# Differential attention in a two-layer trunk: the query split on all 128 partitions into a tile of its own, and eight copies in place of four

## The reference

```python
q, k, v = jnp.split(u @ w_in, 3, axis=-1)
q = apply_rope(q.reshape(bsz, seq, DIFF_HEADS, 2, DIFF_DH), cos, sin)   # 8 heads, 2 components of 64
k = apply_rope(k.reshape(bsz, seq, DIFF_HEADS, 2, DIFF_DH), cos, sin)
...
s = jnp.einsum('bhcqd,bhckd->bhcqk', qb, k).astype(jnp.float32) * scale
p = jax.nn.softmax(jnp.where(mask, s, -jnp.inf), axis=-1)               # causal mask
a = p[:, :, 0] - lam_val * p[:, :, 1]
return jnp.einsum('bhqk,bhkv->bhqv', a.astype(v.dtype), v)
```

## Time and profile before

| what | value |
|---|---|
| runs | 2237.3, 2237.4, 2239.85 us, median 2237.4 |
| profiled execution | 2239.56 us, of which the span of the trace is 2237.8 us |
| mean granted TensorE clock | 0.998 of 2.4 GHz |
| busy of PE, VectorE, ScalarE, GpSimd | 99%, 73%, 43%, 39% of the span |
| chain of waits that ended last | PE 95%, VectorE 3%, ScalarE 1% |
| attention | about 1078 to 1540 us of the span, 56.9 us a head |

### The profile page before, as it was taken

How to read it: one execution, slowest core, us unless ns; L and a number is a source line. 1 busy time by engine, 2 the same in 40 slices (tenths; PEclk the granted TensorE clock), 3 DMA queues, 4 the chain that set the end, 5 groups by cost and what they waited for, 6 DMA issues and landing times.

```text
span 2237.8 us, 28701 instructions
## 1 busy us (share of the span) xinstructions
PE 2208.1 (99%) x10501; PEld 1836.4 (82%) x10501; DVE 1638.5 (73%) x2141; ACT 973.3 (43%) x1613; POOL 874.3 (39%) x805
## 2 busy tenths in 40 slices
PE   8999999999999999999999999999999999999998
PEld 6888888888888888888888888877888888888887
DVE  6877776599669478399577777786599569388397
ACT  6354454354244243345254445564354243343346
POOL 4945546200234233230866666675201234232320
PEclk9999999999999999999999999999999999999999
DMA  8677743463551632701522222222463542633601
GB/s 256 217 269 259 244 155 99 139 246 113 188 188 43 254 128 103 269 13 38 160 67 66 66 66 66 66 76 76 160 230 109 200 176 75 245 113 123 234 0 76
DMA packets 139844, 317.37 MB, mean 142 GB/s; under 512 B 8609, under 2 KB 82514, under 8 KB 126546
## 3 DMA queue, kind: packets, MB, share of 16 engines
q1 hardware_dynamic: 137552, 315.78, 40.9%
q10 hardware_dynamic: 2178, 0.06, 0.1%
HBM read 242.41 MB, written 56.62 MB: 134 GB/s over the span
## 4 chain that ended last, share of the span: by engine, by line
PE 95%; DVE 3%; ACT 1%; issue 1%; DMA 0%; ACTq 0%; DVEq 0%
PE aps L1317 10%; PE aps L1321 10%; PE aps L1319 10%; PE mps L1317 4%; PE dps L1317 4%; PE mps L1321 4%; PE dps L1321 4%; PE mps L1319 4%; PE dps L1319 4%; PE dps L1183 4%; PE dps L1185 4%; PE dps L1184 4%; PE dps L1201 3%; PE dps L1203 3%; PE dps L1202 3%; PE mps L1676 2%
## 5 line engine op out<-in xcount | busy, mean ns | idle before, releaser
L1317 PE MATMUL aps<-b_ring,w_hi 128*128 128x512 f32 x640 | 249.3, 390 | 0.0
L1321 PE MATMUL aps<-b_ring,w_hi 128*128 128x512 f32 x640 | 249.0, 389 | 0.0
L1319 PE MATMUL aps<-b_ring,w_lo 128*128 128x512 f32 x640 | 249.0, 389 | 0.0
L1031 POOL TENSOR_TENSOR s_blk<-s_blk,a 128x1024 f32<-128x1024 f32 x24 | 68.6, 2860 | 380.1 <-DVE w_lo L2520 253.8
L2538 DVE TENSOR_TENSOR b_ring<-h,b_ring 128x1024 fp32r<-128x1024 f32 x120 | 206.5, 1728 | 5.6 <-ACT b_ring L1914 5.6
L909 POOL TENSOR_TENSOR w_hi<-w_raw,ones 128x256 fp32r<-128x256 f32 (+1 forms) x133 | 122.7, 952 | 201.1 <-PE dps L1203 103.9
L1023 POOL TENSOR_TENSOR s_blk<-a,a22u 128x1024 f32<-128x1024 f32 x12 | 35.5, 2960 | 325.6 <-DMA a<-in_w_up 318.6
L1317 PE MATMUL aps<-b_ring,a_hi 128*128 128x512 f32 x384 | 149.8, 390 | 0.0
L1319 PE MATMUL aps<-b_ring,a_lo 128*128 128x512 f32 x384 | 149.4, 389 | 0.0
L1321 PE MATMUL aps<-b_ring,a_hi 128*128 128x512 f32 x384 | 149.4, 389 | 0.0
L1317 PEld LDWEIGHTS aps<-b_ring,w_hi 128*128 128x128 f32 x640 | 120.1, 188 | 25.4 <-issue 0.7
(11 more groups left out here) (514 smaller groups left out, 6362.5 us busy)
## 6 DMA issues: line engine op xcount, KB each, us to landing
b_ring<-xs SPq DMA_DIRECT2D x42, 2048.0 KB, 7.9
xs<-b_ring SPq DMA_DIRECT2D x14, 2048.0 KB, 7.9
one_hi<-xm SPq DMA_DIRECT2D x19, 1024.0 KB, 5.0
one_lo<-xm SPq DMA_DIRECT2D x19, 1024.0 KB, 7.3
a<-in_w_up SPq DMA_DIRECT2D x16, 1024.0 KB, 5.3
a<-in_w_down SPq DMA_DIRECT2D x16, 1024.0 KB, 7.9
w_raw<-in_diff_w_in SPq DMA_DIRECT2D x24, 512.0 KB, 4.0
mix_a<-in_mlstm_w_in SPq DMA_DIRECT2D x36, 256.0 KB, 7.8
```

The lines of the kernel that those rows point to most:

```text
L1317: nc.tensor.matmul(to[:, n], wh, ring[:, 0, k], start=new and k == 0, stop=False, skip_group_check=not new)
L1319: nc.tensor.matmul(to[:, n], wl, ring[:, 0, k], start=False, stop=False, skip_group_check=not new)
L1321: last = nc.tensor.matmul(to[:, n], wh, ring[:, 1, k], start=False, stop=(k == 3), skip_group_check=not new)
```

## The change

A new tile `qn` of 128 partitions by 2 by 1024 holds the high part (`qn[:, 0]`) and the low part (`qn[:, 1]`) of the queries, each component in the half where it lies in `a_next`. ScalarE writes the high part by one instruction on 128 partitions, VectorE the low part by another. SP then copies, for each part and each component c, the half of `qn` that holds it into both halves of `q_hi[:, c]` or `q_lo[:, c]`: eight copies of 256 KB per head in place of four. PE waits for all eight. The semaphore `qk_hi` counts three per head instead of four. The keys are split as before.

```diff
--- before.py
+++ after.py
@@ -321,6 +321,7 @@
             k_st = sb("k_st", [P, 2, S], f32r, stack=s)
             ee = sb("ee", [P, 2, S], stack=s)
             at = sb("at", [P, NB, P], stack=s)
+            qn = sb("qn", [P, 2, S], f32r, stack=s)
         rings = {j: sb(f"b_ring{j}", [P, 2, 4, HALF], f32r) for j in (0, 2, 1)}
         b_ring = [rings[j] for j in range(3)]
 
@@ -580,12 +581,14 @@
 
             def repeat_q(hd):
 
-                sp.wait_ge(qk_hi, 4 * hd + 2)
-                for c in range(2):
-                    sp.dma_start(q_hi[MAP[1 - c], c].bitcast(f32), q_hi[MAP[c], c].bitcast(f32)).then_inc(q_repeated, 16)
-                sp.wait_ge(q_lo_ready, hd + 1)
-                for c in range(2):
-                    sp.dma_start(q_lo[MAP[1 - c], c].bitcast(f32), q_lo[MAP[c], c].bitcast(f32)).then_inc(q_repeated, 16)
+                for part, dst in ((0, q_hi), (1, q_lo)):
+                    if part == 0:
+                        sp.wait_ge(qk_hi, 3 * hd + 1)
+                    else:
+                        sp.wait_ge(q_lo_ready, hd + 1)
+                    for c in range(2):
+                        for half in range(2):
+                            sp.dma_start(dst[MAP[half], c].bitcast(f32), qn[MAP[c], part].bitcast(f32)).then_inc(q_repeated, 16)
 
             def staged(i, p):
 
@@ -1630,7 +1633,7 @@
             def attention_start(hd, feed=lambda n: None, first=False):
 
 
-                pe.wait_ge(q_repeated, 64 * hd + 64)
+                pe.wait_ge(q_repeated, 128 * hd + 128)
                 pe.wait_ge(qk_ready, hd + 1)
                 scores(hd, 0, first)
                 feed(FEED)
@@ -2285,11 +2288,10 @@
             first_high_part(2)
             first_high_part(3)
 
-            def split_q(hd, c):
-
-                if c == 0:
-                    act.wait_ge(rot_ready, 2 * hd + 1)
-                nc.scalar.activation(q_hi[MAP[c], c], a_next[MAP[c], 0], ACT.Copy).then_inc(qk_hi, 1)
+            def split_q(hd):
+
+                act.wait_ge(rot_ready, 2 * hd + 1)
+                nc.scalar.activation(qn[:, 0], a_next[:, 0], ACT.Copy).then_inc(qk_hi, 1)
 
             def split_k(hd):
                 act.wait_ge(rot_ready, 2 * hd + 2)
@@ -2332,7 +2334,7 @@
                 elif more:
                     split_k(hd + 1)
                 if s == NB - 1 and more:
-                    split_q(hd + 1, 0)
+                    split_q(hd + 1)
                 act.wait_ge(pv_done, n + 1)
                 if m == 0 and follows:
                     act.wait_ge(oy_done, hd)
@@ -2341,9 +2343,6 @@
                 nc.scalar.activation(acc[:, m % 2, 0:P], mps[:, 0, 3 * P:4 * P], ACT.Square,
                                      scale=small[:, 11, m:m + 1],
                                      accum_out=small[:, 3, m:m + 1]).then_inc(o_out, 1)
-                if s == NB - 1 and more:
-                    split_q(hd + 1, 1)
-
             def early_highs(t):
 
                 act.wait_ge(oy_out, 2 * (t + 1))
@@ -2365,8 +2364,7 @@
                     attention_start(hd + 1)
                     step(hd + 1, 1)
 
-            for c in range(2):
-                split_q(0, c)
+            split_q(0)
             split_k(0)
             attention_start(0)
             step(0, 1, follows=False)
@@ -3194,17 +3192,14 @@
 
             def split_q(hd):
 
+                dve.wait_ge(qk_hi, 3 * hd + 1)
+                nc.vector.tensor_tensor(qn[:, 1], a_next[:, 0], qn[:, 0].bitcast(f32), ALU.subtract).then_inc(q_lo_ready, 1)
+                dve.wait_ge(q_lo_ready, hd + 1)
+
+            def split_k(hd):
+
                 for c in range(2):
-                    dve.wait_ge(qk_hi, 4 * hd + c + 1)
-                    last = nc.vector.tensor_tensor(q_lo[MAP[c], c], a_next[MAP[c], 0],
-                                                   q_hi[MAP[c], c].bitcast(f32), ALU.subtract)
-                last.then_inc(q_lo_ready, 1)
-                dve.wait_ge(q_lo_ready, hd + 1)
-
-            def split_k(hd):
-
-                for c in range(2):
-                    dve.wait_ge(qk_hi, 4 * hd + c + 3)
+                    dve.wait_ge(qk_hi, 3 * hd + c + 2)
                     last = nc.vector.tensor_tensor(k_st[MAP[1 - c], c], a_next[MAP[c], 1],
                                                    k_st[MAP[c], c].bitcast(f32), ALU.subtract)
                 last.then_inc(qk_ready, 1)
```

## The result

**Slower by 1.6%.** The changed kernel takes 2272.9 us (median of 5 runs) against 2237.9 us for the kernel before (6 runs); the ratio is 1.0156, with a 95% interval of 1.0145 to 1.0166. A sixth run took 2773.1 us, with TensorE's mean granted clock at 0.751 over the whole program, and is left out of median and ratio (with it the median is 2274.1). Against the 2237.4 us from which the forecast was made the ratio gives 2272.3 us; the forecast was 2265.3 us with a range of 2249 to 2273. So the direction and the mechanism came out, and the size lies at the very top of the range.

The account below looks back on a forecast made before the run. TensorE bounds the kernel, busy 2208.1 of 2237.8 us. Waits for copies, 3 x 4.0 + 3 x 2.6 + 0.6 = 20.4 us, plus 7.5 us of clock, added to 2237.4 give 2265.3 us; range 2249 to 2273.

Parts of the forecast that it names:

- The slack of 0.2 us and who is late next: At a head change the last low query copy lands about 0.2 us before PE is ready; later copies make PE wait.
- The rate (1.11 us a copy, 8.9 us of flow): Each head's eight 256 KB query copies flow at 233 GB/s, 8.9 us instead of 4.5.
- Odd heads 4.0 us: At heads 1, 3 and 5 the queries flow behind a weight panel, so PE waits 4.0 us each.
- Even heads 2.6 us: At heads 2, 4 and 6 nothing flows ahead and the issue moves 1.67 us earlier; PE waits 2.6 us each.
- The last head, 0.6 us: At head 7 copies land at 1491.0 against PE's start at 1488.92; PE's work ends 0.6 us later.
- The ScalarE and VectorE terms at nothing: Single splits save 1.05 us of ScalarE and one of two VectorE subtractions per head, but bring no gain in time.
- a fall in the three odd heads and in two of the three even ones: 5 x 1.5 = 7.5 us, none in the last: TensorE's clock falls behind five of the head-change waits, 1.5 us each, adding 7.5 us.
- None in the last: No clock fall in head 7, since its idle 1.44 us brought none in the trace before.
- Rival 4: Copies within a half at 214 GB/s, clock falls at all seven head changes, 1.7 us each: 2272.4 us; chance 0.05.

Follow-up runs that it names:

- x8_same: Kernel before plus four unread 256 KB query copies per head, each within its half of the partitions, PE waiting for all eight: 2288.1 us (ratio 1.0223).
- x8_cross: As x8_same, but each spare copy goes from one half of the partitions into the other: 2289.1 us (ratio 1.0234).
- a4_cross_only: Changed kernel with the four copies within a half left out from head 1 on, only the crossing ones kept: 2238.1 us (ratio 0.9996).
- wide_extra: Kernel before plus 1 MB of spare traffic per head as two 512 KB copies on all 128 partitions: 2267.4 us (ratio 1.0119).
- early_split: Changed kernel, all eight copies, with splits and copy issue moved earlier, for odd heads ahead of the weight panel: 2240.5 us (ratio 1.0006).

## Why the prediction was right, and where it was short

- **The slack of 0.2 us and who is late next: right.** One further copy brings 1.1 us of wait, so next to nothing was in hand.
- **The rate (1.11 us a copy, 8.9 us of flow): right within 4%.** 8.6 us at odd heads, 9.2 at even ones. (By its own reading, four copies in 4.5 us, a copy takes 1.125 us and eight take 9.0.) A copy within a half costs the same as one across, which the prediction had assumed and x8_same against x8_cross shows.
- **Odd heads 4.0 us: right** (3.99, 4.00, 3.78). **Even heads 2.6 us: short** by 0.4 (2.95 to 3.03). The flow was 0.3 us longer than taken, and the last copy landed some 1.4 us behind its data, not 1.2.
- **The last head, 0.6 us: right for the waits, and 1.7 us short by the clock.** The wait was 3.17 us instead of 0.61, so 2.56 us were lost ahead of its first scores (2.08 by the landing forecast at 1491.0; the copies came another 0.5 us later). Behind that point 0.3 us net were won back: the later wait of 1.44 us went, and a fall of the clock took 1.71. VectorE indeed was at its square roots until 1525.2, 2.9 us behind the moment at which PE was ready (1522.32), but had to wait another 0.93 us, until 1526.11, for the scores. The head's net is 2.3 us, and without the fall it is about the 0.6 forecast.
- **The ScalarE and VectorE terms at nothing: right.** a4_cross_only is at the time of before.
- **The step that failed is the clock's, "a fall in the three odd heads and in two of the three even ones: 5 x 1.5 = 7.5 us, none in the last".** There were falls at all seven heads, of 1.71 us (the low clock lasts 3.4 us, not 3), one of them double: 13.7 us, 12.2 of them outside PE's waits. The runs with fewer copies show what the trace of before could not. At heads 1 to 6, waits of 1.1 us brought no fall; waits of 2.2 us brought one at four of six; waits of 2.9 us and more (the changed kernel, x8_same, x8_cross and wide_extra) at 24 of 24, and those of 4.8 us mostly cost twice as much. The five falls assumed would have suited waits of 2.2 us, not of 3.0.
- **"None in the last" rested on one execution.** The 1.44 us idle of the earlier trace rows brought no fall there, but one of 1.48 us at the same place brought one in a4_cross_only and in early_split. Of the nine traces seven fall in the last head; beside the kernel before, only wide_extra doesn't, behind a wait of 2.98 us. What decides it there is open.
- The Trainium skill ("TensorE: Matmul & The Clock Gate", Part 1) is named there for this: waits for DMA between bursts of products bring the throttled clock back. The changed kernel's trace agrees, at seven heads of seven. What the prediction doesn't say is that the Trainium skill ties it to the length of the idle. The runs agree with that in kind: at heads 1 to 6 none of the waits of 1.1 us brought a fall, four of the six waits of 2.2 us did, and all of 2.9 us and more.
- **Rival 4** gave the time best, 2272.4 us, by its seven falls at 1.7 us. Its other half, copies slowed within a half, is shown not to be, so its closeness is in part luck.
- **That the time lies inside the range is by 0.7 us** (2272.3 against 2273), and the top of the range came from rival 4 and not from the forecast's own sum: the mechanism was foreseen, the size only just. Of the profiled 36 us about 2 belong to the start of the program and not to the change.

## What to carry to other kernels

A copy that nobody waits for in the profile may still have no slack: compare the landing of the last with the start of its reader before adding traffic, and price the addition as flow (bytes by the rate of that shape), not as issues or as operations saved. A wait of PE of 2 us or more in dense work mostly cost 1.7 us of clock on top of itself, and more when it was 4.8 us long, so here such waits counted half as much again (12.2 us beside 23.3). If a new tile frees a split from an old reader, move the work into the idle time this opens; the tile alone doesn't.

## What the runs showed of the hardware that was not expected

- SP's issue seems held back by what is in flight: of the changed kernel's copies of 256 KB the first three are issued 0.5 to 0.7 us apart, the low ones 1.1 us apart (the median of their 32), the pace at which they flow. The four low issues of heads 1 to 6 took 3.9 to 4.5 us of SP. Nobody waited for what stood behind them here.
- A loss by the clock behind these waits was 1.71 us or about 3.42 and nothing between, for waits from 1.5 to 5.1 us; at those of 4.8 us and more it was the larger in 12 of 14.
- The first 50 us of the program vary from one execution to the next. The trace of before lost 3.4 us to the low clock there, that of the changed kernel 8.5, as its window shows; the other runs' profiles 3.4 to 5.1.

```profile
30.00:40.00 10.00, 9.52 (x41) 8.10 (x42) 7.75 (x13) 6.64 (x8) 4.33 (x3) 0.58 0.58 211
40.00:50.00 10.00, 10.00 (x42) 8.31 (x41) 4.57 (x17) 0.10 (x1) 6.91 (x9) 0.73 1.13 301
```

What decides this wasn't tried.
